# Neighbourhood attention on single heads: a lag of two units, values in two column halves, copies shared by ScalarE and VectorE

## Chip, core and metric

The kernel runs on one core of one Trainium2 chip. The metric is the device time of one execution in microseconds, the median of several runs. Engines are called by their short names: PE (TensorE; PEld are its weight loads), DVE (VectorE), ACT (ScalarE), POOL (GpSimd) and SP (SyncE).

## What is computed

Two layers of a hybrid trunk over 128 context tokens and 2048 latent tokens. A layer has one input projection, three parallel mixers (RWKV scans, neighbourhood attention with 6 heads of 64, latent attention with 6 heads) and one output projection. The change concerns the neighbourhood attention of the latent tokens alone. The tokens lie on a grid of 32 rows by 64 columns. A query sees 8 grid rows around its own, in them the columns that a mask lets through, with a bias by relative position, and also 256 keys of a cache without bias:

```python
def row_block(args):
    r, q_r = args
    rs = jnp.clip(r - kr // 2, 0, rows - kr)
    ...
    s_loc = jnp.einsum('bqhd,bjkhd->bhqjk', q_r, k_b) * scale + bias
    s_loc = jnp.where(col_mask[:, None, :], s_loc, NEG_INF).reshape(B, H, GRID_W, kr * GRID_W)
    s_ctx = jnp.einsum('bqhd,bchd->bhqc', q_r, k_ctx) * scale
    p = jax.nn.softmax(jnp.concatenate([s_loc, s_ctx], -1), -1)
    ...
    return (jnp.einsum('bhqjk,bjkhd->bqhd', p_loc, v_b)
            + jnp.einsum('bhqc,bchd->bqhd', p[..., kr * GRID_W:], v_ctx))
```

All of it is in 32-bit floats.

## The kernel before

`build` (L2348) runs its phases one after another, with a barrier between them, in a hardware loop over the two layers. `phase_neighbourhood` (L1464) is one of them.

A unit is one head (of 6) of one query tile (128 queries, two grid rows; 16 tiles): 96 units in a layer. An inner tile (12 of the 16) has 576 local keys (nine grid rows, of which each half of the tile masks one) and 256 cached keys; an edge tile (the first two and the last two) has 512 and 256. Ahead of the units PE, DVE and POOL build the bias tables (L1579 to L1587, L1617, L1536 to L1541).

For each unit the engines do this:

- PE, `score` (L1624): three matmuls (two at the edge) write the scores into `ps_s`, which has room for one unit.
- DVE, `maximum` (L1589): adds the bias to the local scores (L1601) into `scores` in SBUF, copies the cached keys' scores there (L1602), which lets PE go on to the next scores, and takes the maximum with its sign changed (L1604).
- ACT, `exp` (L1555): one exponential over 832 (768) columns into `probs`, which has two buffers.
- PE and ACT, `turn_and_multiply` (L1376) and `to_sbuf` (L1415): PE turns the probabilities in blocks of 128 keys (L1392), four blocks into one bank of `ps_t` and three (two at the edge) into the other; ACT copies all of them into `probsT` (L1566); PE multiplies every turned block with its values (L1404). The values' tile has a 65th column of ones, so that the sum of the probabilities comes with the product.
- DVE, `normalise` (L1430), once for six units: divides by that sum. POOL stores the tile, SP loads the next queries.

The order on PE is written by hand: scores of unit u, then turns and values of unit u-1 (L1654). ACT copies for unit u-1, then does exp of unit u (L1568). All engines run five turns of a hardware loop over pairs of query tiles (`over_queries`, L1332), with the edges outside of it. In it waits are on values in registers, and behind each wait stands `hold` (L90), which counts up a semaphore.

A 32-bit matmul is two passes in the trace (two records with a weight load each); a turn is one.

The latent attention (`phase_latent_attention`, L1927) has another form: static Python loops, a lag of two units, the maximum in two parts straight from PSUM (L2013, L2033), copies divided between ACT (L1995) and DVE (L2008), and values multiplied in two halves of 64 queries each (L2075), which write to partitions 0 to 63 and 64 to 127 of `ps_o`.

Of the kernel before, what the change touches and what calls it, by code (L numbers as in the profile page):

```python
# [25 lines left out]
P = 128  # L26
# [1437 lines left out]
def phase_neighbourhood(core, l):  # L1464


    nc, d, hold = core.nc, core.dram, core.hold
    N_DR = 2 * NA_ROWS - 1
    tiles_in = [(i * P, P) for i in range(4)] + [(4 * P, GRID)] + [(NA_LOCAL + i * P, P) for i in range(2)]
    tiles_edge = [(i * P, P) for i in range(6)]  # L1470
    groups = 2
    with ExitStack() as mem:
        def sb(name, shape):
            return mem.enter_context(nc.sbuf_tensor(name, shape, F32))

# [10 lines left out]
        scores = sb("n_scores", [P, 2, NA_KEYS])  # L1486
        at = Attention(core, mem, "n", 2, NA_KEYS, 1)
        ps_b = [mem.enter_context(nc.psum_tensor(f"n_ps_b{i}", [P, CHUNK // GRID, GRID], F32)) for i in range(2)]
        const_in, ones_done, bias_mm, bias_half, table_done = (core.sem(f"n_{n}") for n in
                                                              ("const_in", "ones_done", "bias_mm", "bias_half", "table_done"))  # L1490
        score_read = core.sem("n_score_read")
        parts = [(h, a, b) for h in range(N_NA) for a, b in ((0, 8), (8, N_DR))]

        with nc.Block() as block:
            @block.sync
            def _(sp):

                sp.wait_ge(ones_done, 3)
                sp.dma_start(at.ident[:, :], d["ident"]).then_inc(const_in, 16)
# [16 lines left out]

                def body(pair, before):
                    for q in pair:
                        if q.t > 1:

                            sp.wait_ge(at.score_done, q.n * UNITS - UNITS)
                            hold(sp, "sp")
                        qn = d["feat_attn"][0:D_NA, bass.ds(q.row, P)].rearrange("(h p) n -> p h n", p=P)
                        for e in range(2):
                            rows = slice(HD * e, HD * e + HD)
                            sp.dma_start(qT[rows, q.p, :, e, :], qn[rows, :, :]).then_inc(at.q_in[q.p], 16)
                over_queries(sp, body)

            @block.gpsimd
            def _(pool):  # L1530
                nc.gpsimd.memset(v[:, :, :, :], 1.0).then_inc(ones_done, 1)
                nc.gpsimd.memset(v_ctx[:, :, :, :], 1.0).then_inc(ones_done, 1)
                nc.gpsimd.memset(qT[:, :, :, :, :], 0.0).then_inc(ones_done, 1)


                pool.wait_ge(bias_half, 2 * len(parts))  # L1536
# [6 lines left out]
                def body(pair, before):  # L1543
                    for q in pair:
                        pool.wait_ge(at.out_done, q.n + 1)
                        hold(pool, "pool")
                        pool.dma_start(d["mix_tok"][bass.ds(q.row, P), D_RWKV:D_RWKV + D_NA], at.out[:, q.p, :, :]
                                       .rearrange("p h e -> p (h e)")).then_inc(at.out_sent[q.p], 16)
                over_queries(pool, body)
                for p in range(2):  # L1550
                    pool.wait_ge(at.out_sent[p], 8 * NQ)

            @block.scalar
            def _(act):
                def exp(u):  # L1555

                    act.wait_ge(at.max_done, u.n + 1)
                    hold(act, "act")
                    keys = NA_KEYS if u.q.edge is None else NA_KEYS - GRID
                    nc.scalar.activation(at.probs[:, u.p, 0:keys], scores[:, u.p, 0:keys], ACT.Exp,  # L1560
                                         bias=at.stat[:, u.p:u.p + 1]).then_inc(at.exp_done, 1)

                def move(u):
                    tiles = tiles_in if u.q.edge is None else tiles_edge
                    for g in range(groups):
                        at.to_sbuf(act, "act", lambda o, i: nc.scalar.activation(o, i, ACT.Copy), u, g, groups, tiles)  # L1566

                def body(pair, before):  # L1568
                    for u, last in units_of(pair, before):
                        if last:  # L1570
                            move(last)
                        exp(u)
                move(Unit(over_queries(act, body), UNITS - 1))

            @block.vector
            def _(dve):


                dve.wait_ge(const_in, 16 * (9 + NQ))  # L1579
                for i, (h, a, b) in enumerate(parts):  # L1580
                    dve.wait_ge(bias_mm, i + 1)
                    for e in range(2):
                        rows = slice(GRID * e, GRID * e + GRID)
                        nc.vector.tensor_tensor(bias[rows, h, a + e:b + e, :], ps_b[i % 2][rows, 0:b - a, :],
                                                col_mask[rows, :].unsqueeze(1).broadcast_to([GRID, b - a, GRID]),
                                                ALU.add).then_inc(bias_half, 1)
                dve.wait_ge(table_done, 1)  # L1587

                def maximum(u):  # L1589

                    dve.wait_ge(at.score_done, u.n + 1)
                    hold(dve, "dve")
                    if u.q.t > 0 or u.h > 1:

                        dve.wait_ge(at.exp_done, u.n - 1)
                        hold(dve, "dve")
                    edge = u.q.edge
                    local = NA_LOCAL if edge is None else NA_LOCAL - GRID
                    keys = local + PAST
                    table = bias_in[:, u.h, :] if edge is None else bias[:, u.h, edge:edge + 8, :].rearrange("p m c -> p (m c)")  # L1600
# [6 lines left out]
                def body(pair, before):  # L1607
                    for u, last in units_of(pair, before):
                        maximum(u)
                        if last and u.h == 0:  # L1610
                            at.normalise(dve, last.q)
                at.normalise(dve, over_queries(dve, body))

            @block.tensor
            def _(pe):
                pe.wait_ge(const_in, 16 * (9 + NQ))
                for i, (h, a, b) in enumerate(parts):  # L1617
                    if i >= 2:

                        pe.wait_ge(bias_half, 2 * (i - 1))  # L1620
                    nc.tensor.matmul(ps_b[i % 2][:, 0:b - a, :], flip[:, :], windows[:, h * N_DR + a:h * N_DR + b, :],
                                     start=True, stop=True).then_inc(bias_mm, 1)

                def score(u):  # L1624
                    q = u.q
                    if u.h == 0:
                        pe.wait_ge(at.q_in[q.p], same_parity(q, 32) + 32)
                        hold(pe, "pe")
                    if not u.first:

                        pe.wait_ge(score_read, u.n)
                        hold(pe, "pe")
                    lhs = qT[:, q.p, u.h // 2, u.h % 2, :]
                    blocks = 9 if q.edge is None else 8
                    key = q.first * P
                    nc.tensor.matmul(at.ps_s[:, 0:CHUNK], lhs, kT[:, u.h // 2, bass.ds(key, CHUNK)], start=True, stop=True)
                    if blocks == 9:
                        nc.tensor.matmul(at.ps_s[:, CHUNK:NA_LOCAL], lhs, kT[:, u.h // 2, bass.ds(key + CHUNK, GRID)], start=True, stop=True)
                    nc.tensor.matmul(at.ps_s[:, blocks * GRID:blocks * GRID + PAST], lhs, kT_ctx[:, u.h // 2, :],
                                     start=True, stop=True).then_inc(at.score_done, 1)  # L1640

                def values(u):
                    q = u.q
                    n_local = 5 if q.edge is None else 4
                    tiles = tiles_in if q.edge is None else tiles_edge

                    def v_of(k):
                        if k >= n_local:
                            return v_ctx[:, k - n_local, u.h, :]
                        width = tiles[k][1]  # L1650
                        return v[0:width, bass.ds(q.first + k, 1), u.h, :].rearrange("p a e -> p (a e)")
                    at.turn_and_multiply(pe, u, u.first, tiles, groups, v_of)

                def body(pair, before):  # L1654
                    for u, last in units_of(pair, before):
                        score(u)
                        if last:
                            values(last)
                values(Unit(over_queries(pe, body), UNITS - 1))
# [829 lines left out]
```

## Time and profile before

| | |
|---|---|
| median of 3 runs | 8927.61 us (8922.58 to 8949.45) |
| the profiled execution | 8935.97 us |
| its span, first to last instruction | 8934.5 us |
| PE busy | 7394.6 us, 83% of the span |
| DVE, ACT, POOL busy | 3297.0, 2315.3, 2091.5 us |
| mean granted PE clock | 0.893 of full speed |

The profiled execution is one run, 8 us above the median. Busy time counts instructions at work. An idle stretch of an engine is put down to what ended it. Matmul ends are modelled, and a matmul's own length says little where many follow closely: what counts is the distance of their starts. The rows that matter here are those of the neighbourhood phase, and of the latent attention for the forms of work that the neighbourhood phase doesn't have yet.

### The profile page before, as it was taken

To read this page: it belongs to the slowest core of one execution; us is meant where nothing else is said; L and a number is where in the kernel's file an instruction comes from. 1 tells how busy PE (TensorE), PEld (TensorE's weight loads), DVE (VectorE), ACT (ScalarE), POOL (GpSimd) and SP (SyncE) were. 2 spreads that over 40 slices of the span, in tenths; PEclk is the share of its full clock that TensorE was granted. 3 is DMA by queue.
4 is the path that set the end of the run, shared out by engine and by line. 5 is a ranking of instruction groups with operands and counts; after the bars stand their busy time and mean duration, and the time that the engine had idled before them with its cause. 6 is when DMAs were issued, how large, how long until landed. Compare 5 with 4: busy or idle time off the path is not lost. (4 is left out here: it accounts for less than half of the span.)

```text
span 8934.5 us, 141036 instructions
## 1 busy us (share of the span) xinstructions
PE 7394.6 (83%) x55540; PEld 5240.5 (59%) x55540; DVE 3297.0 (37%) x4888; ACT 2315.3 (26%) x3968; POOL 2091.5 (23%) x1804
## 2 busy tenths in 40 slices
PE   6999688888838857999889996888787487599989
PEld 2444377787726635667444444777777265367654
DVE  0111244434434443444211112434443444444433
ACT  0111122222204423555111111222221133245531
POOL 0000267756610000000000004666664100000000
PEclk9999888878759978999999997878978699799999
DMA  6111100000030010000431111000001200100013
GB/s 229 49 47 41 50 17 19 21 21 14 17 94 14 13 42 21 12 11 9 161 116 47 42 46 43 14 21 21 14 21 47 62 14 19 42 13 11 12 64 126
DMA packets 387793, 379.32 MB, mean 42 GB/s; under 512 B 86294, under 2 KB 329494, under 8 KB 385998
## 3 DMA queue, kind: packets, MB, share of 16 engines
q1 hardware_dynamic: 360912, 295.42, 11.5%
q0 software_dynamic: 17552, 67.25, 2.4%
q8 instruction: 426, 6.98, 0.3%
q10 hardware_dynamic: 8816, 8.96, 0.3%
q14 instruction: 87, 0.71, 0.0%
HBM read 246.05 MB, written 134.41 MB: 43 GB/s over the span
## 5 line engine op out<-in xcount | busy, mean ns | idle before, releaser
L502 PE MATMUL a_ps_p<-a_w,a_hT 128*128 128x512 f32 (+1 forms) x3808 | 1607.0, 582 | 8.8 <-DVE a_hT L417 8.8
L502 PEld LDWEIGHTS a_ps_p<-a_w,a_hT 128*128 128x128 f32 x3808 | 719.4, 190 | 858.7 <-issue 858.7
L2046 PE MATMUL t_ps_s<-l_kT_all,t_qT 96*128 96x512 f32 (+1 forms) x1920 | 930.0, 567 | 27.8 <-DMA t_qT<-mla_q 15.5
L2061 PEld LDWEIGHTS t_ps_t<-t_ident,t_probs 128*128 128x128 f32 x3456 | 436.6, 141 | 423.0 <-issue 398.9
L2013 DVE TENSOR_REDUCE t_part<-t_ps_s 128x1 f32<-128x1536 f32 (+1 forms) x384 | 521.2, 1358 | 392.6 <-PE t_ps_s L2046 392.6
L1139 PE MATMUL s_ps<-s_YT,s_X 128*128 128x128 f32 x2720 | 366.6, 291 | 248.4 <-DVE s_YT L1004 248.4
L802 POOL TENSOR_TENSOR s_lev<-s_Araw,s_wide 128x512 f32<-128x512 f32 x340 | 510.9, 1537 | 157.4 <-ACT s_Araw L875 157.4
L1988 ACT ACTIVATE t_probs<-t_ps_s,t_stat 128x1024 f32<-128x1024 f32 (+1 forms) x576 | 476.6, 898 | 252.7 <-DVE t_stat L2033 252.7
L2061 PE MATMUL t_ps_t<-t_ident,t_probs 128*128 128x128 f32 x3456 | 535.6, 273 | 2.4 <-DVE t_probsT L2008 1.4
L1139 PEld LDWEIGHTS s_ps<-s_YT,s_X 128*128 128x128 f32 x2720 | 338.8, 203 | 276.9 <-issue 276.9
L380 ACT ACTIVATE a_proj<-a_ps_p 128x512 f32<-128x512 f32 (+1 forms) x238 | 139.4, 586 | 1372.9 <-PE a_ps_p L502 1372.9
L1995 ACT ACTIVATE t_probsT<-t_ps_t 128x512 f32<-128x512 f32 x576 | 343.5, 597 | 574.0 <-PE t_ps_t L2061 574.0
L2331 PE MATMUL e_ps_y<-e_w,e_mT 128*128 128x512 f32 x1088 | 478.0, 598 | 13.8 <-DMA e_w<-w_out 13.8
L833 POOL MEMSET s_M<- 128x512 f32 x2 | 1.0, 524 | 1941.4 <-POOLq L88 1941.4
L2075 PE MATMUL t_ps_o<-l_v_all,t_probsT 128*64 128x65 f32 x13824 | 445.3, 223 | 0.0
L2075 PEld LDWEIGHTS t_ps_o<-l_v_all,t_probsT 128*64 128x64 f32 x13824 | 418.7, 138 | 32.2 <-issue 32.2
L1976 POOL DMA_DIRECT2D mix_tok<-t_out x32 | 17.4, 544 | 1689.2 <-DVE t_out L2021 1689.2
L875 ACT ACTIVATE s_YT<-s_ps 128x512 f32<-128x512 f32 x170 | 101.5, 597 | 1090.6 <-PE s_ps L1139 1090.6
L1009 DVE TENSOR_TENSOR s_XT<-s_XT,s_ps 128x512 f32<-128x512 f32 x340 | 218.5, 684 | 438.3 <-PE s_ps L1139 438.3
L1139 PEld LDWEIGHTS s_ps<-s_XT,s_lev 128*128 128x128 f32 x2720 | 356.4, 210 | 30.9 <-issue 24.8
L1139 PE MATMUL s_ps<-s_XT,s_lev 128*128 128x128 f32 x2720 | 373.8, 296 | 0.0
L2008 DVE COPY t_probsT<-t_ps_t 128x512 f32<-128x512 f32 (+1 forms) x384 | 212.5, 553 | 430.7 <-PE t_ps_t L2061 430.2
(287 smaller groups left out, 12836.3 us busy)
## 6 DMA issues: line engine op xcount, KB each, us to landing
s_raw<-feat_rwkv SPq DMA_DIRECT2D x68, 390.0 KB, 3.5
m_w<-w_mod SPq DMA_DIRECT2D x12, 2048.0 KB, 8.0
a_w<-w_in SPq DMA_DIRECT2D x12, 2048.0 KB, 18.7
feat_attn<-a_fT SPq DMA_DIRECT2D x34, 576.0 KB, 5.9
a_x<-stream SPq DMA_DIRECT2D x34, 512.0 KB, 3.6
e_x<-stream POOLq DMA_DIRECT2D x34, 512.0 KB, 6.3
e_mix<-mix_tok SPq DMA_DIRECT2D x34, 512.0 KB, 5.6
e_gates<-gate_tok SPq DMA_DIRECT2D x34, 512.0 KB, 6.8
```

The lines of the kernel that those rows point to most:

```text
L502: mm = nc.tensor.matmul(ps_p[c % 4][:, 0:hi - lo], hT[:, k, :], w[:, k, lo:hi], start=(k == 0), stop=(k == KD - 1))
L802: last = mask_pair(lambda o, i, m: tt(o, i, m, ALU.mult), e, lev[:, j, :, :, :], Araw[:, e, :, :], W_LEV + 1 + j)
L1009: tt(row, row, ps[:, 2 + e, :], ALU.add).then_inc(S("xt_added"), 1)
L1139: last = mm(out(e, dh), left[:, e, dh, :], right(e, dh), start=True, stop=True)
L1988: nc.scalar.activation(probs[:, u % 2, lo:hi], ps_s[:, lo:hi], ACT.Exp, bias=stat[:, u % 2:u % 2 + 1]).then_inc(exp_done, 1)
L1995: nc.scalar.activation(probsT[:, b[0]:b[-1] + 1, :], bank(u, g)[:, 0:len(b), :], ACT.Copy).then_inc(moved_a, 1)
L2008: nc.vector.tensor_copy(probsT[:, b[0]:b[-1] + 1, :], bank(u, g)[:, 0:len(b), :]).then_inc(moved_v, 1)
L2013: nc.vector.tensor_reduce(part[:, u % 2, i:i + 1], ps_s[:, lo:hi], AX, ALU.max)
L2046: mm = nc.tensor.matmul(ps_s[:, lo:hi], qT[:, q % 2, h, :], keys.kT[:, h, lo:hi], start=True, stop=True)
L2061: tr = nc.tensor.transpose(bank(u, g)[:, i, :], probs[:, u % 2, k * P:(k + 1) * P], ident[:, :])
L2075: mm = nc.tensor.matmul(ps_o[c:c + HD, h, :], probsT[:, k, c:c + HD], keys.v[:, k, h, :], start=(k == 0), stop=(k == n_blk - 1))
L2331: mm = nc.tensor.matmul(ps_y[tile.p][i][:, :], mT[:, tile.p, k, :], w[:, k, i * CHUNK:(i + 1) * CHUNK], start=(k == 0), stop=(k == KD - 1))
```

## The change

`phase_neighbourhood` is written anew in the form of the latent attention; nothing else is touched. It no longer uses `Attention`, `over_queries` or `hold`; all loops over units are static.

- PE at step i: turns of unit i-2, scores of unit i, values of unit i-2. `ps_s` has two buffers, and scores wait for exp of the unit two before. The bias tables' PSUM lies inside these buffers.
- Values: each turned block is multiplied in two halves of 64 columns. The half block at the end of an inner tile goes last, over 128 rows, in a slot of `probsT` whose lower half POOL has cleared.
- DVE at step i: copies the second bank of turned blocks of unit i-2, then takes the maximum of unit i: of the cached keys straight from PSUM, then one operation that adds the bias and continues the maximum, then the change of sign.
- ACT at step i: exp of unit i-1 (cached keys from PSUM, local ones from SBUF), then the copy of the first bank of unit i-2.

```diff
+        scores = sb("n_scores", [P, 2, NA_LOCAL])
+        probsT = sb("n_probsT", [P, 7, P])
+        ps_s = [mem.enter_context(nc.psum_tensor(f"n_ps_s{i}", [P, 2 * CHUNK], F32)) for i in range(2)]
+        ps_b = [ps_s[i][:, 0:CHUNK].rearrange("p (m c) -> p m c", c=GRID) for i in range(2)]
...
+                for q in range(NQ):
+                    if q > 1:
+                        sp.wait_ge(score_done, (q - 1) * UNITS)
...
+                nc.gpsimd.memset(probsT[:, :, :], 0.0).then_inc(zero_done, 1)
...
                 def exp(u):
-                    act.wait_ge(at.max_done, u.n + 1)
-                    hold(act, "act")
-                    nc.scalar.activation(at.probs[:, u.p, 0:keys], scores[:, u.p, 0:keys], ACT.Exp,
-                                         bias=at.stat[:, u.p:u.p + 1]).then_inc(at.exp_done, 1)
+                    local = shape_of(u // UNITS)[2]
+                    act.wait_ge(max_done, u + 1)
+                    if u >= 2:
+                        act.wait_ge(turn_done, (u - 1) * 2)
+                    bias_u = stat[:, u % 2:u % 2 + 1]
+                    nc.scalar.activation(probs[:, u % 2, local:local + PAST], ps_s[u % 2][:, local:local + PAST], ACT.Exp, bias=bias_u)
+                    nc.scalar.activation(probs[:, u % 2, 0:local], scores[:, u % 2, 0:local], ACT.Exp, bias=bias_u).then_inc(exp_done, 1)
                 def move(u):
+                    act.wait_ge(turn_done, u * 2 + 1)
+                    nc.scalar.activation(probsT[:, 0:4, :], ps_t[0][:, :, :], ACT.Copy).then_inc(moved_a, 1)
+                for i in range(U + 2):
+                    if 1 <= i <= U:
+                        exp(i - 1)
+                    if i >= 2:
+                        move(i - 2)
...
                 def maximum(u):
-                    nc.vector.tensor_tensor(scores[:, u.p, 0:local], at.ps_s[:, 0:local], table, ALU.add)
-                    nc.vector.tensor_copy(scores[:, u.p, local:keys], at.ps_s[:, local:keys]).then_inc(score_read, 1)
                     dve.drain()
-                    nc.vector.tensor_reduce(at.stat[:, u.p:u.p + 1], scores[:, u.p, 0:keys], AX, ALU.max, negate=True)\
-                        .then_inc(at.max_done, 1)
+                    dve.wait_ge(score_done, u + 1)
+                    if u >= 2:
+                        dve.wait_ge(exp_done, u - 1)
+                    nc.vector.tensor_reduce(part[:, u % 2, 0:1], ps_s[u % 2][:, local:local + PAST], AX, ALU.max)
+                    dve.drain()
+                    nc.vector.tensor_tensor_reduce(out=scores[:, u % 2, 0:local], in0=ps_s[u % 2][:, 0:local], in1=table, scale=1.0,
+                                                   scalar=part[:, u % 2, 0:1], op0=ALU.add, op1=ALU.max,
+                                                   accum_out=part[:, u % 2, 1:2])
+                    dve.drain()
+                    nc.vector.tensor_scalar(stat[:, u % 2:u % 2 + 1], part[:, u % 2, 1:2], -1.0, None, ALU.mult).then_inc(max_done, 1)
+                def move(u):
+                    dve.wait_ge(turn_done, u * 2 + 2)
+                    last = nc.vector.tensor_copy(probsT[:, 4:6, :], ps_t[1][:, 0:2, :])
+                    if inner:
+                        last = nc.vector.tensor_copy(probsT[0:GRID, 6, :], ps_t[1][0:GRID, 2, :])
+                    last.then_inc(moved_v, 1)
+                for i in range(U + 3):
+                    if i >= 3 and (i - 3) % UNITS == UNITS - 1:
+                        normalise((i - 3) // UNITS)
+                    if 2 <= i < U + 2:
+                        move(i - 2)
+                    if i < U:
+                        maximum(i)
...
+                def values(u):
+                    pe.wait_ge(moved_a, u + 1)
+                    blocks = [(k, v[:, first + k, h, :]) for k in range(4)] + [(4 + k, v_ctx[:, k, h, :]) for k in range(2)]
+                    if edge is None:
+                        blocks.append((6, v[:, first + 4, h, :]))
+                    for k, (slot, rows) in enumerate(blocks):
+                        if slot == 4:
+                            pe.wait_ge(moved_v, u + 1)
+                        for c in (0, HD):
+                            mm = nc.tensor.matmul(ps_o[c:c + HD, h, :], probsT[:, slot, c:c + HD], rows,
+                                                  start=(k == 0), stop=(k == len(blocks) - 1))
+                for i in range(U + 2):
+                    if i >= 2:
+                        turn(i - 2)
+                    if i < U:
+                        score(i)
+                    if i >= 2:
+                        values(i - 2)
```

PE's `turn(u)` waits for exp of unit u and, ahead of each of the two banks, for the copy of unit u-1 out of it; `score(u)` waits for exp of unit u-2.

## Rows read from the trace of the kernel before

**Rows 1.** Windows: stretch, length, busy PE PEld DVE ACT POOL, clock, DMA, GB/s.

```profile
2664.90:3136.00 471.10, 406.85 (x2468) 318.23 (x2468) 210.63 (x318) 189.25 (x361) 8.21 (x15) 0.98 0.04 13
3430.00:4260.00 830.00, 806.25 (x9598) 562.69 (x9596) 386.12 (x512) 409.89 (x576) 9.79 (x18) 0.98 0.05 14
7064.50:7536.40 471.90, 406.80 (x2468) 318.10 (x2468) 211.39 (x320) 189.22 (x361) 8.31 (x16) 0.98 0.04 13
```

**Rows 2.** Waits, 2880 to 3078 us: who for whom, us in all, times, longest.

```profile
PE n_ps_o L1404 <- ACT n_probsT L1566: 25.3, 40, 0.9
```

**Rows 3.** Timeline, one inner unit: start, us, engine, line, operation, count, idle before.

```profile
2880.73 1.44 PE L1404 MATMUL n_ps_o<-n_v,n_probsT 128*128 x10 [0.54 <-ACT n_probsT L1566]
...
2882.60 1.08 PE L1636 MATMUL n_ps_s<-n_kT,n_qT 128*128 x2
...
2883.68 0.65 PE L1639 MATMUL n_ps_s<-n_kT_ctx,n_qT 128*128 128x256 f32 x2
...
2884.16 0.93 PE L1392 MATMUL n_ps_t<-n_ident,n_probs 128*128 128x128 f32 x7
2884.59 0.76 DVE L1601 TENSOR_TENSOR n_scores<-n_ps_s,n_bias_in 128x576 f32<-128x576 f32 x1 [2.70 <-PE n_ps_s L1639]
2884.89 1.02 ACT L1566 ACTIVATE n_probsT<-n_ps_t 128x512 f32<-128x512 f32 x3 [1.89 <-PE n_ps_t L1392]
...
2885.63 1.44 PE L1404 MATMUL n_ps_o<-n_v,n_probsT 128*128 x10 [0.54 <-ACT n_probsT L1566]
```

**Rows 4.** Timeline, PE in one edge unit.

```profile
3092.76 1.08 PE L1636 MATMUL n_ps_s<-n_kT,n_qT 128*128 128x512 f32 x2
...
3093.68 0.59 PE L1639 MATMUL n_ps_s<-n_kT_ctx,n_qT 128*128 128x256 f32 x2
...
3094.11 0.82 PE L1392 MATMUL n_ps_t<-n_ident,n_probs 128*128 128x128 f32 x6
...
3096.94 1.08 PE L1636 MATMUL n_ps_s<-n_kT,n_qT 128*128 128x512 f32 x2
```

**Rows 5.** Timeline, latent attention, end of one unit and start of the next.

```profile
3562.31 0.60 ACT L1995 ACTIVATE t_probsT<-t_ps_t 128x512 f32<-128x512 f32 x1 [0.70 <-PE t_ps_t L2061]
...
3562.54 0.38 PE L2061 MATMUL t_ps_t<-t_ident,t_probs 128*128 128x128 f32 x2
...
3562.86 2.32 PE L2075 MATMUL t_ps_o<-l_v_all,t_probsT 128*64 128x65 f32 x72
3563.78 0.15 DVE L2033 TENSOR_REDUCE t_stat<-t_part 128x1 f32<-128x2 f32 x1
...
3563.97 2.48 ACT L1988 ACTIVATE t_probs<-t_ps_s,t_stat 128x1024 f32<-128x1024 f32 x3 [1.06 <-DVE t_stat L2033]
...
3565.14 1.13 PE L2046 MATMUL t_ps_s<-l_kT_all,t_qT 96*128 96x512 f32 x2
...
3566.10 0.60 PE L2061 MATMUL t_ps_t<-t_ident,t_probs 128*128 128x128 f32 x4
...
3566.54 1.02 PE L2046 MATMUL t_ps_s<-l_kT_all,t_qT 96*128 96x512 f32 x2
```

**Rows 6.** Groups by shape, latent attention: count, busy us, mean ns, idle before.

```profile
L1988 ACT ACTIVATE t_probs<-t_ps_s,t_stat 128x1024 f32<-128x1024 f32 x182 | 192.8, 1110 | 103.5 <-DVE t_stat L2033 103.5
...
L2013 DVE TENSOR_REDUCE t_part<-t_ps_s 128x1 f32<-128x1536 f32 x91 | 159.9, 1758 | 139.5 <-PE t_ps_s L2046 139.5
L2013 DVE TENSOR_REDUCE t_part<-t_ps_s 128x1 f32<-128x768 f32 x91 | 87.1, 958 | 37.7 <-PE t_ps_s L2046 37.7
...
L1988 ACT ACTIVATE t_probs<-t_ps_s,t_stat 128x256 f32<-128x256 f32 x90 | 42.7, 474 | 0.0
L2008 DVE COPY t_probsT<-t_ps_t 128x256 f32<-128x256 f32 x90 | 37.4, 415 | 0.2 <-issue 0.2
```

**Rows 7.** Groups by shape, neighbourhood phase of the first layer.

```profile
L1560 ACT ACTIVATE n_probs<-n_scores,n_stat 128x832 f32<-128x832 f32 x72 | 71.1, 988 | 72.7 <-DVE n_stat L1604 72.7
...
L1533 POOL MEMSET n_qT<- 128x1536 f32 x1 | 1.4, 1380 | 0.0
```

More of the change, by code:

```diff
@@ L1464, in phase_neighbourhood @@
 def phase_neighbourhood(core, l):
-    nc, d, hold = core.nc, core.dram, core.hold
+    nc, d = core.nc, core.dram
     N_DR = 2 * NA_ROWS - 1
-    tiles_in = [(i * P, P) for i in range(4)] + [(4 * P, GRID)] + [(NA_LOCAL + i * P, P) for i in range(2)]
-    tiles_edge = [(i * P, P) for i in range(6)]
-    groups = 2
+    U = NQ * UNITS
     with ExitStack() as mem:
@@ L1515, in _ @@
                                      .rearrange("p (h e) -> p h e", e=HD)).then_inc(const_in, 16)
[L1517 to L1527, printed above, removed]
+                for q in range(NQ):
+                    if q > 1:
+                        sp.wait_ge(score_done, (q - 1) * UNITS)
+                    qn = d["feat_attn"][0:D_NA, CTX + q * P:CTX + (q + 1) * P].rearrange("(h p) n -> p h n", p=P)
+                    for e in range(2):
+                        half = slice(HD * e, HD * e + HD)
+                        sp.dma_start(qT[half, q % 2, :, e, :], qn[half, :, :]).then_inc(q_in[q % 2], 16)
             @block.gpsimd
@@ L1541, in _ @@
                 nc.gpsimd.memset(bi[GRID:P, :, 0, :], NEG).then_inc(table_done, 1)
[L1543 to L1549, printed above, removed]
+                for q in range(NQ):
+                    pool.wait_ge(out_done, q + 1)
+                    pool.dma_start(d["mix_tok"][CTX + q * P:CTX + (q + 1) * P, D_RWKV:D_RWKV + D_NA], out[:, q % 2, :, :]
+                                   .rearrange("p h e -> p (h e)")).then_inc(out_sent[q % 2], 16)
                 for p in range(2):
-                    pool.wait_ge(at.out_sent[p], 8 * NQ)
+                    pool.wait_ge(out_sent[p], 8 * NQ)
             @block.scalar
@@ L1555, in exp @@
                 def exp(u):
-                    act.wait_ge(at.max_done, u.n + 1)
-                    hold(act, "act")
-                    keys = NA_KEYS if u.q.edge is None else NA_KEYS - GRID
-                    nc.scalar.activation(at.probs[:, u.p, 0:keys], scores[:, u.p, 0:keys], ACT.Exp,
-                                         bias=at.stat[:, u.p:u.p + 1]).then_inc(at.exp_done, 1)
-                def move(u):
[L1564 to L1573, printed above, removed]
+                    local = shape_of(u // UNITS)[2]
[5 more added lines that the diff above has]
+                    nc.scalar.activation(probs[:, u % 2, 0:local], scores[:, u % 2, 0:local], ACT.Exp, bias=bias_u).then_inc(exp_done, 1)
+                def move(u):
+                    act.wait_ge(turn_done, u * 2 + 1)
+                    nc.scalar.activation(probsT[:, 0:4, :], ps_t[0][:, :, :], ACT.Copy).then_inc(moved_a, 1)
+                act.wait_ge(zero_done, 1)
+                for i in range(U + 2):
[3 more added lines that the diff above has]
+                        move(i - 2)
             @block.vector
@@ L1586, in _ @@
                                                 ALU.add).then_inc(bias_half, 1)
                 dve.wait_ge(table_done, 1)
+                dve.wait_ge(zero_done, 1)
                 def maximum(u):
[L1591 to L1598, printed above, removed]
@@ L1607, in body @@
[L1607 to L1612, printed above, removed]
+                    q, h = u // UNITS, u % UNITS
+                    _, edge, local = shape_of(q)
+                    dve.wait_ge(score_done, u + 1)
+                    if u >= 2:
+                        dve.wait_ge(exp_done, u - 1)
@@ L1622, in _ @@
                                      start=True, stop=True).then_inc(bias_mm, 1)
+                pe.wait_ge(bias_half, 2 * len(parts))
                 def score(u):
[L1625 to L1640, printed above, removed]
@@ L1642, in values @@
-                def values(u):
[L1643 to L1659, printed above, removed]
+                    q, h = u // UNITS, u % UNITS
+                    first, edge, local = shape_of(q)
+                    if h == 0:
+                        pe.wait_ge(q_in[q % 2], 32 * (q // 2 + 1))
+                    if u >= 2:
+                        pe.wait_ge(exp_done, u - 1)
@@ new lines, in turn @@
+                def turn(u):
+                    _, edge, local = shape_of(u // UNITS)
+                    pe.wait_ge(exp_done, u + 1)
+                    if u > 0:
+                        pe.wait_ge(moved_a, u)
+                    p = probs[:, u % 2, :]
+                    for k in range(4):
+                        tr = nc.tensor.transpose(ps_t[0][:, k, :], p[:, k * P:(k + 1) * P], ident[:, :])
+                    tr.then_inc(turn_done, 1)
+                    if u > 0:
+                        pe.wait_ge(moved_v, u)
+                    for k in range(2):
+                        tr = nc.tensor.transpose(ps_t[1][:, k, :], p[:, local + k * P:local + (k + 1) * P], ident[:, :])
+                    if edge is None:
+                        tr = nc.tensor.transpose(ps_t[1][0:GRID, 2, :], p[:, 4 * P:4 * P + GRID], ident[:, :])
+                    tr.then_inc(turn_done, 1)
```

55 lines of the change are left out of this document (43 added, 12 removed).

## Prediction

> **What bounds the kernel now.** I read the windows first [rows 1]. The neighbourhood loop takes 471 us in each of the two layers; in it PE has work for 407 us, DVE and ACT for 211 and 189 us, at a granted clock of 0.98, the 2.4 GHz level but for the start. So PE sets the pace and the other engines are idle more than half of the time. The list of waits then says what PE itself waits for: ACT's copy of the turned probabilities, 40 times in 198 us, 25 us in all, 0.63 us a unit [rows 2]. The timeline of one inner unit gives PE's order [rows 3]: values start at 2880.73, the scores of the next unit at 2882.60 (values cost 1.87 us), the turns at 2884.16 (scores 1.56 us), the next values at 2885.63 (1.47 us, of which the seven turns need half; the rest is the wait for ACT's copies). Together 4.90 us for this unit. An edge unit takes 4.18 us, with scores at 3092.76, turns at 3094.11 (1.35 us) and the next scores at 3096.94 [rows 4]. Take from this: PE's own order turn, wait, values is the stall, and values are the dearest part of PE's work.
>
> The new phase is built like the latent attention that is already in this kernel (L1927 to L2087): lag of two units, static Python loops, partial maxima, DVE and ACT sharing the copies, values in two halves of 64 columns. In that phase PE is busy 806 of 830 us [rows 1], so its rows price nearly every part.
>
> **PE's work in a new unit.**
> - Turns: four cost 0.44 us up to the next scores (3566.10 to 3566.54) [rows 5], 0.11 each; seven cost 0.77, six at the edge 0.66.
> - Scores: same three matmuls, 1.56 and 1.35 us [rows 3, 4].
> - Values: 14 passes with 128-column weights become 28 with 64-column weights (the half block at the end is now multiplied over 128 rows, half of them zeros, in no more passes). 72 such passes took 2.28 us (3562.86 to 3565.14), 0.0317 each [rows 5]; 28 cost 0.89, 24 cost 0.76. Before, one of the 14 cost 1.87/14 = 0.134. This takes 0.98 us off every inner unit.
> - Going into the halves: two turns need 0.22 us, but the values came 0.32 us after them [rows 5], so 0.10 for the change. I allow the same on the way out. This row speaks for a drain at each change of shape; the Trainium skill, TensorEngine Tiling (Array Packing), Key Properties, says that changing the tiling mode drains the engine, which the 0.10 us agrees with. Without that drain the sum would be 0.20 us a unit lower, about 38 us in all.
>
> PE's sum: 0.77 + 1.56 + 0.10 + 0.89 + 0.10 = 3.42 us, edge 0.66 + 1.35 + 0.10 + 0.76 + 0.10 = 2.97 us. The stall is gone from it, since the scores of unit i (1.56 us) stand between turn and values and cover a copy of 0.60 us.
>
> **What is late next: a loop over two units.** ACT runs exp(i-1) before it moves unit i-2, so values(i-2) wait for the maximum of i-1. Followed round: values(i-2), turn(i-1), scores(i+1), DVE's maximum(i+1), exp(i+1), move(i), values(i), two units later. Its price, inner unit:
> - values and change 0.99, turns 0.77, scores from first start to last end 1.73 (2883.68 + 0.65 - 2882.60) [rows 3];
> - hand-over 0.04 to DVE, as DVE to ACT in the latent phase (3563.78 + 0.15 to 3563.97) [rows 5];
> - maximum of 256 scores in PSUM: 768 took 0.958 and 1536 took 1.758 [rows 6], 1.04 ns an element, so 0.43; gap 0.08;
> - addition with a running maximum over 576: no row shows this operation. Below it is the plain addition over the same operands, 0.76 [rows 3]; above it is the addition and a separate maximum over 576, 0.76 + 0.08 + 0.76 = 1.60, by the slope above. I take 0.76: it streams the same elements once, and the addition is the nearest row. Gap 0.08, then the change of sign as dear as a two-element maximum, 0.16 [rows 5];
> - hand-over 0.04; exp of 256 from PSUM 0.47 [rows 6], of 576 from SBUF 0.99 [rows 7] less 256 x 0.83 ns (the slope of the two L1988 rows) = 0.78; successive ACT operations overlap by 0.10 (three pieces took 2.48, not 2.69) [rows 5, 6], so 1.15; move 0.60 less 0.10 [rows 5];
> - hand-over to PE 0.14 (2884.89 + 0.60 to 2885.63) [rows 3, 5].
>
> Sum 6.87 us for two units, 3.43 us each; for edge units (24 passes, six turns, scores 1.51 us, 512 elements in addition and exp) 6.29, 3.15 each. So loop and PE are level for inner units, and the loop is 0.2 us longer at the edge. I take 3.43 and 3.15.
>
> **The rest of the edits.** DVE gets the copies of two and a half blocks back (0.42 for 256 columns [rows 6], some 0.28 by the slope for the 64-row one) and loses the copy of 256 (0.42) and the maximum over 832; its unit is 0.43 + 0.76 + 0.16 + 0.69 + gaps, about 2.4 us of 3.4. The copies stand ahead of maximum(i) on its queue: they wait for turn(i-2), which PE has finished 1.5 us before scores(i) end, and take 0.8 us, so maximum(i) is not held up. Was the cover gone, it would be 0.8 us in the loop, 0.4 a unit. ACT's unit is about 1.7 us. PE's new wait at the head of each unit, for exp(i-2), has scores(i) and values(i-2) queued behind it; in the loop above exp(i-2) is done about 1.6 us before. SP's query loads are as many as before and start six units ahead. POOL's clearing of probsT (896 columns against 1.4 us for 1536 [rows 7]) runs before SP's loads have landed; uncovered it is 0.8 us a layer. Scores 0 now wait for the last bias half, but DVE waits for POOL's table anyway. Unrolling costs nothing I can see: the latent phase is unrolled too and keeps PE at 806 of 830 us [rows 1]; bounds of it are a gain (the register waits and counters go, 0.26 us from scores to DVE, 2883.68 + 0.65 to 2884.59 [rows 3]) and the loss in the rival on hand-overs. The score buffer's wait moves from DVE's read of the unit before to exp of the unit before that: not late.
>
> **Sum.** 72 x 3.43 + 24 x 3.15 = 322.6 us a layer. For filling and emptying the pipeline and PE's start at half clock I add 6 us, an estimate: the first maximum and exp take 1.5 + 1.25, the clock of 0.98 over 471 us [rows 1] means about 9 us at half speed, 4.5 lost, and the last two units have no scores behind them, which gives 2.7 back. 471.5 - 328.6 = 143 us a layer, 285 in all. The profiled execution took 8935.97 us with a span of 8934.5, 8 us over the median of 8927.61. So 8651 us by the profile and **8643 us** by the median.
>
> **The rivals.**
> - *The loop is longer than its rows* (8670 to 8745, middle 8699). If the addition with maximum needs two passes' time, 576 elements cost 0.60 us more, the loop 7.47, a unit 3.73 (edge 3.42): 144 x 0.30 + 48 x 0.27 = 56 us more, 8699. Three hand-overs at the 0.26 us of before [rows 3] instead of 0.04, 0.04 and 0.14 give half of 0.56, 0.28 a unit, nearly the same time. For it: PE and loop are level, so each addition to the loop shows at half size; against it: plain additions and single waits show neither. The Trainium skill, Vector Engine (DVE) Microarchitecture Reference, Points that are easy to get wrong, says that the accumulating two-source form runs at half rate when both sources are wide and in SBUF; here one source is in PSUM, so by its words it would not apply, and no row here shows it.
> - *Changes of shape are free and the loop gives way* (8605). 3.2 us a unit, 0.2 x 192 = 38 us less. For it: the 0.10 is one row; against it: the loop stands at 3.43 by itself.
> - *The halves don't run side by side* (slower, 9160). If a pass keeps the 0.134 us of before, 28 cost 3.74 and a unit 0.77 + 1.56 + 0.20 + 3.74 = 6.27 (edge 0.66 + 1.35 + 0.20 + 3.2 = 5.4): 587 us a layer, 116 more than now. It decides from a pass of (4.90 - 2.53)/28 = 0.085 us. Against it stands the same shape at 0.0317 us in the latent phase [rows 5].
> - *The lag doesn't take hold* (slower): if some wait ties unit i to unit i-1, the loop of 6.87 us is paid for every unit, over 9200 us. The waits on even and odd buffers show no such tie; the latent phase is tied in the same way and runs freely.
>
> **Chances and range.** Forecast (8618 to 8668) 0.58, longer loop 0.25, free changes 0.12, halves in series 0.04, no lag 0.01. The range from 8600 to 8745 takes in the first three. A difference of 0.3%, 27 us, is about what the measurement can tell. Faster 0.94, same 0.01, slower 0.05.
>
> **What would show it.** Right: in the neighbourhood stretch of the new profile, PE busy nearly throughout at the upper clock; the stretch 329 us long; a value pass at 0.032 us; scores directly behind turns; waits of DVE for scores near 1 us a unit. Wrong: an addition with maximum well over 0.8 us; PE idle ahead of values for ACT's move (the loop, not PE, is the bound; more than 0.2 us a unit makes it the second case); idle PE ahead of turns for exp (the lag is too short); passes near 0.1 us; idle that ends with nothing the profile names (unrolled code); or a change outside this phase.

## The result and the profile after

The changed kernel takes 8640.76 us (median of 4 runs, 8628.21 to 8665.42); the kernel before 8925.10 (4 runs, 8900.92 to 8949.45). The ratio is 0.968, 95% interval 0.9655 to 0.9711: 284 us less. Its profiled execution took 8628.21 us, with a span of 8626.8.

The windows of the neighbourhood phase after, in the columns of [rows 1], from DVE's first operation behind the bias table to the last division:

```profile
2649.30:2976.40 327.10, 317.02 (x3760) 231.12 (x3760) 196.09 (x584) 156.01 (x289) 8.24 (x15) 0.99 0.06 19
...
6902.30:7229.40 327.10, 317.02 (x3760) 231.15 (x3760) 196.09 (x583) 156.02 (x289) 8.21 (x15) 0.99 0.06 19
```

471.1 and 471.9 us have become 327.1 twice, 289 us in all. PE now works 317 of 327 us where it worked 407 of 471; it stays at the upper clock level but for the start (granted clock 0.99). The profiled executions differ by 308 us; of the 19 that are left, 15.6 lie ahead of the first neighbourhood phase (2664.90 against 2649.30), in work that the change doesn't touch.

The waits of 2700 to 2950 us in the changed kernel (as in [rows 2]):

```profile
ACT n_probs L1566 <- DVE n_stat L1606: 132.2, 74, 2.2
DVE n_part L1600 <- PE n_ps_s L1654: 61.0, 73, 0.9
...
PEld n_ps_o L1686 <- ACT n_probsT L1571: 21.3, 60, 0.7
...
PE n_ps_o L1686 <- ACT n_probsT L1571: 1.0, 4, 0.3
```

The last line answers to [rows 2]: PE's wait for the copies has gone from 25.3 us in 198 to 1.0 in 250. ACT and DVE now wait, 1.8 and 0.8 us each time. The timeline of two units (columns as in [rows 3]; other lines of the engines left out) lets us walk round the loop of the prediction:

```profile
2801.72 0.69 PE L1686 MATMUL n_ps_o<-n_v,n_probsT 128*64 128x65 f32 x16
...
2802.69 0.66 PE L1663 MATMUL n_ps_t<-n_ident,n_probs 128*128 128x128 f32 x4
...
2803.51 1.02 PE L1651 MATMUL n_ps_s<-n_kT,n_qT 128*128 128x512 f32 x2
...
2804.53 0.65 PE L1654 MATMUL n_ps_s<-n_kT_ctx,n_qT 128*128 128x256 f32 x2
...
2805.22 0.42 DVE L1600 TENSOR_REDUCE n_part<-n_ps_s 128x1 f32<-128x256 f32 x1 [0.90 <-PE n_ps_s L1654]
...
2805.76 0.82 DVE L1602 CUSTOM_DVE_ANT_0 n_scores<-n_ps_s,n_bias_in,n_part 128x576 f32<-128x576 f32 x1
...
2806.50 0.08 DVE L1602 DVE_READ_ACCUMULATOR2_ANT n_part<- 128x1 f32 x1
...
2806.66 0.15 DVE L1606 TENSOR_SCALAR n_stat<-n_part 128x1 f32<-128x1 f32 x1
...
2806.85 0.47 ACT L1566 ACTIVATE n_probs<-n_ps_s,n_stat 128x256 f32<-128x256 f32 x1 [1.77 <-DVE n_stat L1606]
...
2807.22 0.76 ACT L1567 ACTIVATE n_probs<-n_scores,n_stat 128x576 f32<-128x576 f32 x1
...
2807.89 0.59 ACT L1571 ACTIVATE n_probsT<-n_ps_t 128x512 f32<-128x512 f32 x1
...
2808.53 0.69 PE L1686 MATMUL n_ps_o<-n_v,n_probsT 128*64 128x65 f32 x16
```

Values 2801.72 to turns 2802.69: 0.97. Turns to scores 2803.51: 0.82. Scores to their last end (2804.53 + 0.65 = 2805.18): 1.67. DVE from 2805.22 to 2806.81: 1.59. ACT from 2806.85 to 2808.48: 1.63. With hand-overs of 0.04, 0.04 and 0.05 the next values but one start at 2808.53: 6.81 us for two units, where 6.87 was forecast.

### The profile page after: what moved, and what is told of

Same layout as the page of the kernel before. It is cut to its first block and busy times, and to the rows that moved or that the text cites. A ratio compares the mean times of both kernels' runs of the same rounds, so it can differ in the third digit from the quotient of the medians.

```text
span 8626.8 us, 143698 instructions
## 1 busy us (share of the span) xinstructions
PE 7202.8 (83%) x58132; PEld 5051.9 (59%) x58132; DVE 3266.1 (38%) x5416; ACT 2249.9 (26%) x3824; POOL 2095.3 (24%) x1806
```

## Experiments

A whole execution moves by tens of microseconds with the clock granted in the scans, which no kernel here touches (over 900 to 1700 us it was 0.86 in the kernel before and 0.79 in two_step_max). So single runs are compared by the **stretch**: in the first layer, from the first operation on `n_stat` to the start of the last division. It is 470.4 us before and 325.7 after; in every run the second layer's stretch lies within 0.6 us of the first's. Periods (inner and edge unit) are distances of successive operations on `n_stat`; before 5.05 (from unit to unit it varies, that of [rows 3] has 4.90) and 4.17, after 3.42 and 3.12.

### Does the loop through ACT set the pace?

**act_moves_first**: ACT copies for unit i-2 first, then does exp of unit i-1, so values(i-2) no longer wait for the maximum of i-1.

```diff
+                    if i >= 2:
+                        move(i - 2)
                     if 1 <= i <= U:
                         exp(i - 1)
-                    if i >= 2:
-                        move(i - 2)
```

> ACT copies unit i-2 before it takes exp of unit i-1; all else as in the changed kernel. Theory (the loop over two units through ACT's order binds, PE's own work is a little shorter): the copy no longer follows the maximum of i-1, the loop falls away, and a unit costs PE's own work, 0.97 + 0.82 + 1.57 = 3.36 us inside and 0.85 + 0.71 + 1.38 = 2.94 us at the edge, against 3.42 and 3.12 in the changed kernel. The neighbourhood stretch (first maximum to last division) then goes from 327.7 to about 321 us in a layer, 13 us in all, 0.15% of the time. Rival (PE alone binds): 327.7 us unchanged.

Measured: 318.8 us; 3.40 and 2.95. (The expectation counts from the first maximum to the end of the last division, 2 us more: its 327.7 and 321 are 325.7 and 319 here.) Time 8631.95 us (median of 6), ratio to before 0.9657 (0.9628 to 0.9685). PE in this kernel:

```profile
2800.37 1.02 PE L1651 MATMUL n_ps_s<-n_kT,n_qT 128*128 128x512 f32 x2
...
2801.40 0.65 PE L1654 MATMUL n_ps_s<-n_kT_ctx,n_qT 128*128 128x256 f32 x2
...
2801.98 0.69 PE L1686 MATMUL n_ps_o<-n_v,n_probsT 128*64 128x65 f32 x16
...
2802.49 0.40 PE L1686 MATMUL n_ps_o<-n_v_ctx,n_probsT 128*64 128x65 f32 x8
...
2802.94 0.66 PE L1663 MATMUL n_ps_t<-n_ident,n_probs 128*128 128x128 f32 x4
...
2803.76 1.02 PE L1651 MATMUL n_ps_s<-n_kT,n_qT 128*128 128x512 f32 x2
...
2805.37 0.69 PE L1686 MATMUL n_ps_o<-n_v,n_probsT 128*64 128x65 f32 x16
```

1.61 + 0.96 + 0.82 = 3.39 us is PE's own unit. So the loop (6.81/2 = 3.405) and PE were level for inner units, and the loop was longer at the edge by 0.17 us. The shorter stretch is shown; in the whole time the 14 us of two layers lie inside the intervals, so that this version is faster than the changed kernel is shown by the trace alone.

**two_step_max** and **act_first_two_step**: the addition with running maximum is taken apart, in ACT's order of the change and in the other one.

```diff
-                    nc.vector.tensor_tensor_reduce(out=scores[:, u % 2, 0:local], ..., op0=ALU.add, op1=ALU.max, ...)
+                    nc.vector.tensor_tensor(scores[:, u % 2, 0:local], ps_s[u % 2][:, 0:local], table, ALU.add)
+                    dve.drain()
+                    nc.vector.tensor_reduce(part[:, u % 2, 1:2], scores[:, u % 2, 0:local], AX, ALU.max)
                     dve.drain()
-                    nc.vector.tensor_scalar(stat[:, u % 2:u % 2 + 1], part[:, u % 2, 1:2], -1.0, None, ALU.mult)...
+                    nc.vector.tensor_reduce(stat[:, u % 2:u % 2 + 1], part[:, u % 2, :], AX, ALU.max, negate=True)...
```

> The one operation that adds the bias and continues the maximum is split into an addition and a maximum over the local keys, then a maximum of the two parts; about 0.68 us more on DVE in each unit. Theory (a loop over two units binds): half of it shows, 3.75 us inside, 3.43 at the edge, the stretch 361 us. First rival (PE alone binds): 328 us. Second rival (DVE's chain is paid in every unit): 3.41 + 0.68, the stretch 393 us.

> Both edits together: ACT copies first, and the maximum in two steps. Theory (the loop exists only by ACT's order): the longer maximum costs nothing, the stretch is that of the run with ACT's copies first, about 321 us. Rival (the maximum binds in another way too): 350 us or more.

Measured: 351.9 us (3.69 and 3.36) and 318.8 (3.40 and 2.95). DVE's chain in two_step_max:

```profile
2802.43 0.42 DVE L1600 TENSOR_REDUCE n_part<-n_ps_s 128x1 f32<-128x256 f32 x1 [0.90 <-PE n_ps_s L1653]
...
2802.77 0.75 DVE L1601 TENSOR_TENSOR n_scores<-n_ps_s,n_bias_in 128x576 f32<-128x576 f32 x1
...
2803.59 0.75 DVE L1603 TENSOR_REDUCE n_part<-n_scores 128x1 f32<-128x576 f32 x1
...
2804.42 0.16 DVE L1605 TENSOR_REDUCE n_stat<-n_part 128x1 f32<-128x2 f32 x1
```

From 2802.43 to 2804.58 are 2.15 us against 1.59 in the changed kernel: 0.56 more, and half of it is the 0.27 that a unit grew by. (The expected 361 us were 9 too many, since they took 0.68 for the 0.56.) With ACT's order turned round the same longer chain costs nothing: 318.8 in both. That is the loop's proof: a time on DVE counts at half its size as long as exp stands ahead of the move, and 0.56 us of it cost nothing in the other order.

### What are the halves worth?

**full_width**: values over 128 columns at once. **full_width_half_mid**: that, and the half block over 64 rows behind the four local blocks, as before the change. **halves_half_mid**: the half block so, but in column halves.

```diff
# full_width
-                        for c in (0, HD):
-                            mm = nc.tensor.matmul(ps_o[c:c + HD, h, :], probsT[:, slot, c:c + HD], rows,
-                                                  start=(k == 0), stop=(k == len(blocks) - 1))
+                        mm = nc.tensor.matmul(ps_o[:, h, :], probsT[:, slot, :], rows,
+                                              start=(k == 0), stop=(k == len(blocks) - 1))
# both with half_mid
+                    if edge is None:
+                        blocks.append((6, GRID, v[0:GRID, first + 4, h, :]))
+                    blocks += [(4 + k, P, v_ctx[:, k, h, :]) for k in range(2)]
...
+                            ... probsT[0:deep, slot, ...], rows, ...
```

> Values multiplied over all 128 columns at once, as before the change; all else as in the changed kernel. Theory (the halves are the larger part of the gain): a pass costs 0.113 us, as in the edge units of before, 14 of them 1.59, PE's unit 0.82 + 1.57 + 1.6 = 4.0 inside and 3.45 at the edge, the stretch 380 us. Rival (the lag and the order gave it all, and weight loads hide behind them): 328 us.

> The values over 128 columns, as in full_width, but the half block is multiplied over 64 rows and in the middle, behind the four local blocks, as the kernel before did. Theory (a change between 128 and 64 rows costs PE): two passes took 0.46 us in before_static where two full ones take 0.22, so 0.24 us more in each inner unit, 3.80 to 4.04, edge 3.36 unchanged, stretch 358.9 + 72 x 0.24 = 376 us. Rival (64 rows cost nothing of their own, and the dearer passes of before come from elsewhere): 3.80 and 358.9.

> The changed kernel with the half block multiplied over 64 rows and in the middle, still in two halves of 64 columns. Theory (a change between 128 and 64 rows costs PE): before_halves_static had 1.26 us of values against 0.97, so 0.29 us more on PE; PE stood at 3.39 us a unit and becomes the bound at 3.68, edge 3.12 unchanged, stretch 325.7 + 72 x 0.26 = 344 us. Rival (64 rows cost nothing of their own): 3.42 and 325.7.

Measured: full_width 358.9 us (3.80 and 3.36), full_width_half_mid 378.5 (4.08 and 3.36), halves_half_mid 344.6 (3.69 and 3.12). The values of one inner unit, up to the next turns (in full_width with the scores on either side as well), in full_width:

```profile
2804.10 0.65 PE L1654 MATMUL n_ps_s<-n_kT_ctx,n_qT 128*128 128x256 f32 x2
2804.59 1.00 PE L1685 MATMUL n_ps_o<-n_v,n_probsT 128*128 128x65 f32 x8
2805.43 0.61 PE L1685 MATMUL n_ps_o<-n_v_ctx,n_probsT 128*128 128x65 f32 x4
2805.87 0.39 PE L1685 MATMUL n_ps_o<-n_v,n_probsT 128*128 128x65 f32 x2
2806.10 0.60 PE L1663 MATMUL n_ps_t<-n_ident,n_probs 128*128 128x128 f32 x4
...
2806.87 1.02 PE L1651 MATMUL n_ps_s<-n_kT,n_qT 128*128 128x512 f32 x2
```

in full_width_half_mid:

```profile
2803.37 1.36 PE L1686 MATMUL n_ps_o<-n_v,n_probsT 128*128 128x65 f32 x10
2804.66 0.66 PE L1686 MATMUL n_ps_o<-n_v_ctx,n_probsT 128*128 128x65 f32 x4
2805.16 0.61 PE L1663 MATMUL n_ps_t<-n_ident,n_probs 128*128 128x128 f32 x4
```

and in halves_half_mid:

```profile
2803.73 0.95 PE L1687 MATMUL n_ps_o<-n_v,n_probsT 128*64 128x65 f32 x20
2804.61 0.45 PE L1687 MATMUL n_ps_o<-n_v_ctx,n_probsT 128*64 128x65 f32 x8
2804.99 0.66 PE L1663 MATMUL n_ps_t<-n_ident,n_probs 128*128 128x128 f32 x4
```

Values take 1.51, 1.79 and 1.26 us; in the changed kernel 0.97. So 14 full passes of 128 rows cost 0.108 each; one block of 64 rows among them costs 0.28 us more, whether in full width or in halves (1.26 - 0.97 = 0.29). Both runs move the half block and shrink it at once, but the starts of the single passes in the trace of full_width_half_mid show where the time lies. Full passes start 0.112 us apart; from the last of them to the first of 64 rows are 0.205, to the second 0.161, to the next full pass 0.202 and to the one behind it 0.160. So each of the two changes between 128 and 64 rows costs 0.14 us, and the place in the order alone costs nothing that shows. The two edits of the values are worth 33 and 19 us a layer, nearly independent of each other: both undone, the stretch is 52.8 longer. My expectation for full_width was 21 us too long: it put 1.59 us for values, 0.82 for turns and 1.57 for scores, rounded up to 4.0, and they take 1.51, 0.77 and 1.52.

### Does the order on PE and DVE matter?

**scores_first**: PE does scores(i), then turns and values of i-2, so scores no longer stand between them. **max_first**: DVE takes the maximum before it copies.

```diff
# scores_first (PE)
-                    if i >= 2:
-                        turn(i - 2)
                     if i < U:
                         score(i)
                     if i >= 2:
+                        turn(i - 2)
                         values(i - 2)
# max_first (DVE)
-                    if 2 <= i < U + 2:
-                        move(i - 2)
                     if i < U:
                         maximum(i)
+                    if 2 <= i < U + 2:
+                        move(i - 2)
```

> PE takes the scores of unit i ahead of the turns of unit i-2, so that values follow turns directly; all else as in the changed kernel. Theory (scores between turns and values cover the copy): PE waits about 0.5 us a unit for the copies, 1.59 + 0.82 + 0.5 + 0.97 = 3.88 us inside and 3.5 at the edge, the stretch 372 us. Rival (the lag of two alone suffices): 328 us.

> DVE takes the maximum of unit i before it copies unit i-2; all else as in the changed kernel. Theory (DVE's order is what keeps its copy out of PE's way): the copy follows scores(i) and the maximum, values of i-2 wait for it, and a unit costs 1.6 (maximum) + 0.65 (copy) + 0.5 (rest of the values) + 0.82 + 1.67 = 5.2 us inside, 4.65 at the edge, the stretch 495 us, more than before the change. Rival (DVE is idle for a third of the time, its order doesn't matter): 328 us.

Measured: 367.6 us (3.87 and 3.53) and 486.0 (5.21 and 4.51). In scores_first, turns, ACT's copy, values:

```profile
2800.80 0.60 PE L1663 MATMUL n_ps_t<-n_ident,n_probs 128*128 128x128 f32 x4
...
2801.44 0.60 ACT L1571 ACTIVATE n_probsT<-n_ps_t 128x512 f32<-128x512 f32 x1 [0.25 <-PE n_ps_t L1663]
...
2802.09 0.69 PE L1686 MATMUL n_ps_o<-n_v,n_probsT 128*64 128x65 f32 x16 [0.36 <-ACT n_probsT L1571]
```

PE is idle for 0.36 us ahead of each unit's values, the stall of [rows 3] in smaller form: a lag of two units alone doesn't remove it, the scores in between do (42 us a layer). In max_first, DVE's chain and what waits for it:

```profile
2802.92 0.42 DVE L1600 TENSOR_REDUCE n_part<-n_ps_s 128x1 f32<-128x256 f32 x1 [3.10 <-PE n_ps_s L1654]
...
2804.43 0.41 DVE L1611 COPY n_probsT<-n_ps_t 128x256 f32<-128x256 f32 x1
...
2804.77 0.27 DVE L1613 COPY n_probsT<-n_ps_t 64x128 f32<-64x128 f32 x1
...
2805.09 0.45 PE L1686 MATMUL n_ps_o<-n_v_ctx,n_probsT 128*64 128x65 f32 x8 [1.59 <-DVE n_probsT L1613]
```

The copies of i-2, whose turns were long done, wait for scores(i) and then for the maximum; PE stands for 1.59 us in the middle of the values, ahead of the cached blocks. This one order would have used up the whole gain of the stretch (486.0 us against 470.4 before the change).

### What of the rest of the old form?

**before_static**: the kernel before with all units of the phase written out, waits on constants and no `hold`. **before_halves_static**: that, and values in column halves (the half block still over 64 rows, in the middle).

```diff
# both, over_queries
-    with eng.Fori(0, NQ // 2 - 3) as j:
-        looped = ...
-        body(looped[1:], looped[0])
...
+    for t in range(0, NQ, 2):
+        body([make(t), make(t + 1)], make(t - 1) if t else None)
# before_halves_static, turn_and_multiply
+                for c in (0, HD):
+                    mm = self.nc.tensor.matmul(self.ps_o[c:c + HD, h, :], self.probsT[0:width, k, c:c + HD], v_of(k), ...
```

> The kernel before, with the loops over units unrolled in this phase and the counting behind each wait left out; order, lag and values as before. Theory (part of the gain is the static program): waits hand over some 0.2 us sooner and values inside cost as at the edge (0.113 us a pass, 1.59 instead of 1.87 us), 4.4 us inside and 4.0 at the edge, the stretch 424 us instead of 472. Rival (unrolling gives nothing by itself): 472 us.

> As the unrolled kernel before, and with the values in two halves of 64 columns. Theory: values fall from 1.59 to 0.97 us inside (1.36 to 0.85 at the edge) and PE pays for them in full, 3.85 and 3.5 us, the stretch 372 us; what is then left to the changed kernel (328 us) is the lag, the order and the shared copies. Rival (the halves need the lag to be of use): 424 us as without them.

Measured: 440.3 us (4.75 and 4.02) and 386.9 (4.17 and 3.53). In before_static:

```profile
2800.28 1.47 PE L1400 MATMUL n_ps_o<-n_v,n_probsT 128*128 128x65 f32 x10 [0.36 <-ACT n_probsT L1562]
...
2801.43 0.99 ACT L1556 ACTIVATE n_probs<-n_scores,n_stat 128x832 f32<-128x832 f32 x1 [0.78 <-DVE n_stat L1600]
...
2802.17 1.08 PE L1632 MATMUL n_ps_s<-n_kT,n_qT 128*128 128x512 f32 x2
...
2803.25 0.65 PE L1635 MATMUL n_ps_s<-n_kT_ctx,n_qT 128*128 128x256 f32 x2
...
2803.74 0.93 PE L1388 MATMUL n_ps_t<-n_ident,n_probs 128*128 128x128 f32 x7
2803.94 0.76 DVE L1597 TENSOR_TENSOR n_scores<-n_ps_s,n_bias_in 128x576 f32<-128x576 f32 x1 [2.55 <-PE n_ps_s L1635]
...
2805.03 0.55 PE L1400 MATMUL n_ps_o<-n_v,n_probsT 128*128 128x65 f32 x3 [0.36 <-ACT n_probsT L1562]
```

Scores end at 2803.90 and DVE starts at 2803.94: the hand-over of 0.26 us [rows 3] has become 0.04. The 30 us a layer lie elsewhere, though: exp is done at 2802.42, 1.3 us ahead of the turns that need it, so DVE's chain holds nothing up. They lie where PE does wait, between the turns and the next values. This distance is 1.29 us here (2803.74 to 2805.03) against 1.47 in the unit of [rows 3], with PE idle for 0.36 us ahead of the values instead of 0.54; over all units of the layer it sums to 124.1 us against 149.7, 25.6 of the 30. In the kernel before it is 1.47 us in most units outside the hardware loop, which have constants in their waits already but `hold` behind them, and 1.47 to 1.87 inside. So some 0.18 us a unit goes with `hold`; whether the loop itself or its register waits cost the rest, these runs don't tell apart.

The values still cost 1.89 us (2800.28 to 2802.17), so it was not the addresses in registers that made their passes dear, as I had supposed for this run; full_width_half_mid above names the cause for 0.28 of it. Both expectations of this section, 424 and 372 us, left these 0.28 us a unit out, 20 us a layer, and were 16 and 15 us too short.

So the stretch goes, one edit at a time: 470.4, written out without `hold` 440.3 (30 less), column halves 386.9 (53), lag, order, shared copies and split maximum 344.6 (42; the distance to halves_half_mid), half block last over 128 rows 325.7 (19). The shares belong to this order of the edits: in the new form the halves are worth 34 us (378.5 to 344.6) and not 53.

## Why the prediction was right

**The bound and the loop.** Right. The loop of two units measured 6.81 us against 6.87, PE's unit 3.39 against 3.42, the edge 3.12 against 3.15, and act_moves_first and two_step_max show that the loop is what it was said to be. The loop's terms miss by up to 0.09 us and cancel, which is luck: DVE's chain took 1.59 where 1.51 was summed and turns 0.82 for 0.77, but scores 1.67 for 1.73 and the three hand-overs 0.13 for 0.22. Of the 6 us for filling and emptying 6.0 are found (327.1 - 72 x 3.42 - 24 x 3.12), and there too one term was misread: a mean clock of 0.98 over 471 us [rows 1] means about 9 us lost and 19 us at half speed, not 4.5 and 9. The 0.99 of the changed kernel means about 3 lost, so the 4.5 was not far off. That the whole time came within 3 us of 8643 is luck as well, since single runs of the changed kernel lie up to 37 us apart; the stretch is the fairer test, 327.1 us where 328.6 was forecast.

**The addition with maximum**, the one operation without a row, taken at 0.76 between 0.76 and 1.60. The list of operations on its tile, with the shortest, median and longest duration in ns:

```profile
L1602 DVE DVE_READ_ACCUMULATOR2_ANT n_part<- x192: 81/84/85, 2650.5 to 7224.0; 128x1 f32 x192
...
L1602 DVE CUSTOM_DVE_ANT_0 n_scores<-n_ps_s,n_bias_in,n_part x144: 816/818/820, 2689.3 to 7185.4; 128x576 f32<-128x576 f32 x144
L1602 DVE CUSTOM_DVE_ANT_0 n_scores<-n_ps_s,n_bias,n_part x48: 750/751/753, 2649.8 to 7223.3; 128x512 f32<-128x512 f32 x48
```

818 - 751 ns for 64 elements are 1.04 ns an element, as for a plain maximum [rows 6]: one pass. The rival of two passes' time falls. The half rate that the Trainium skill, Vector Engine (DVE) Microarchitecture Reference, Points that are easy to get wrong, gives for two wide sources in SBUF was not seen; one source here is in PSUM, no run had both in SBUF, and that this instruction (`CUSTOM_DVE_ANT_0` in the trace) is of the page's form is not shown. The term was 0.05 too small with the read of the accumulator (1.05 with the sign, 1.00 forecast); the hand-over to PE of 0.05 instead of 0.14 paid for it.

**The halves don't run in series**: 16 passes from 2801.98 to 2802.49 in act_moves_first are 0.032 us each, as in [rows 5].

**Changes of shape.** Their 0.20 us a unit was right in sum (0.21) and not in its parts. Against full_width the changed kernel has 0.05 us more from turns to scores (0.82 against 0.77) and 0.09 more from the cached keys' scores to the values (0.58 against 0.49, in act_moves_first and full_width); the rest is the 0.07 by which the values (0.96) exceed 28 x 0.0317.

**The values: the step that was mis-sized.** "This takes 0.98 us off every inner unit" put the whole of 1.87 - 0.89 down to the halves. The values did go to 0.97, 0.90 less, but the halves give 0.54 of it (1.51 to 0.97), the half block that moved to the end over 128 rows 0.28 (1.79 to 1.51), and 0.08 came with the rest. The edit "in no more passes", which I costed at nothing, is worth 19 us a layer. It didn't hurt the forecast, since the new unit was summed up from rows of the new form, and not as the old unit less each edit.

**"Unrolling costs nothing I can see"**: it gains, 0.30 us in an inner unit of before_static. That its bound below nothing, 0.26 us from scores to DVE, is close to this is chance: the gain lies between turns and values. In the new loop the hand-over to DVE, 0.04 by the latent phase's row, measured 0.04; the one to PE, 0.14 by the old rows, 0.05.

**The copies ahead of the maximum**: "not held up" is right, DVE waits 0.90 us for scores all the same; the other order costs 160 us a layer. **The score buffer and the clearing of `probsT`** show no stall: neither stands among the waits of 2700 to 2950 us, nor the clearing, which runs ahead of the units, among those of 2600 to 2700.

**A mark that can be misread.** "PE idle ahead of values for ACT's move, more than 0.2 us" was to show the second case. The weight loads do wait there, 0.35 us a unit (21.3 us, 60 times), but they wait as long in act_moves_first (0.33, put down to issue), where no loop binds: weights are loaded while the scores still run. Only the matmuls' own wait counts, 1.0 us in all. Read so, the mark works: in two_step_max, where the loop binds with 3.69 us a unit, that wait is 13.9 us from 2700 to 2900 us, 0.26 a unit:

```profile
PE n_ps_o L1685 <- ACT n_probsT L1571: 13.9, 30, 0.8
```

## What to carry to other kernels

Where another phase already has the form that a change brings in, sum the new unit from that phase's rows and walk its loops in each engine's order; what each edit contributes is a second question, and the difference of the old and the new row doesn't answer it. Ask of every in-order engine whether what it does first could wait for a younger unit: here DVE's order decided 160 us a layer, PE's 42 and ACT's 7. A chain in a loop over two units counts at half its length, and only for what stands above the busiest engine's own work.

## What the runs showed of the hardware

- A block of 64 rows among blocks of 128 costs 0.28 us more per unit (two full-width passes; 0.29 for four half-width ones) although it multiplies fewer rows, 0.14 at each of the two changes. The Trainium skill, TensorE: Matmul & The Clock Gate, LDWEIGHTS (loading the stationary operand), says that the time to load weights goes by their columns and not by their rows; the runs agree that fewer rows save nothing, but by this alone the block would cost nothing extra. The Trainium skill, TensorEngine Tiling (Array Packing), Key Properties, says that changing the tiling mode drains the engine; the 0.14 us at each change would fit that, though the runs show the time and not the drain.
- Two column halves of 64 take 0.064 us together (16 passes in 0.51 us) where one pass of 128 columns takes 0.108 (14 in 1.51), with 65 columns streamed in each.
- With `hold` behind the wait, DVE starts 0.26 us after PE's last score, inside the hardware loop [rows 3] as well as in units outside it, whose waits are on constants (2748.34 + 0.65 to 2749.25 in the kernel before). Written out without `hold`, it starts after 0.04 us.
